# Sharing out the taps of a depthwise convolution: which of GpSimd's products it makes itself, and when VectorE does its own

## The reference, cut to what matters

```python
h = rmsnorm(x, mix_norm)
z = h @ w_in                      # q 1024, k 128, v 128, conv 2 x 1024, gates 2 x 1024
q = partial_rope(rmsnorm(zq.reshape(B, S, 16, 64), q_norm), cos, sin)
k = partial_rope(rmsnorm(zk.reshape(B, S, 2, 64), k_norm), cos, sin)
a = sliding_window_attention(q, k, v, sinks) @ attn_proj

ca, cb = jnp.split(zc, 2, axis=-1)
u = ca * jax.nn.sigmoid(cb)
u = causal_depthwise_conv(u, dw_w, dw_b)       # 31 taps for each of 1024 channels
c = jax.nn.silu(layernorm(u, conv_ln_g, conv_ln_b)) @ conv_proj
merged = jax.nn.sigmoid(ga) * a + jax.nn.sigmoid(gb) * c
x = x + merged @ w_out
```

## Time and profile before

| | before |
|---|---|
| median of 3 runs | 1446.55 us |
| profiled execution, its own time | 1445.92 us |
| its span in the trace | 1444.1 us |
| mean granted clock of TensorE | 0.982 |
| TensorE busy | 1365.7 us (95% of the span) |
| VectorE / ScalarE / GpSimd busy | 961.5 / 786.8 / 141.9 us |
| chain that ended last, by engine | PE 78%, DVE 9%, ACT 6%, DMA 3%, POOL 2% |

### The profile page before, as it was taken

One profiled execution on the slowest core, in us unless ns is written; L12 is line 12 of the kernel. 1 busy time (PEld: TensorE's weight loads), 2 busy tenths in 40 slices (PEclk: granted clock), 3 DMA queues, 4 the chain that ended last, 5 costly groups with the idle time before them and its releaser, 6 DMA issues.

```text
span 1444.1 us, 17190 instructions
## 1 busy us (share of the span) xinstructions
PE 1365.7 (95%) x6482; PEld 1127.0 (78%) x6482; DVE 961.5 (67%) x1397; ACT 786.8 (54%) x1250; POOL 141.9 (10%) x166
## 2 busy tenths in 40 slices
PE   6999999849998999999899999899999999899998
PEld 5788788738876887878778888678888888688886
DVE  4776746797867776774877666648875546665543
ACT  5444447858874654444764444666545664654442
POOL 3000102643430010010001000000000000000000
PEclk9999999969999999999999999999999999999999
DMA  9888755613343588875558876545544344566562
GB/s 256 301 264 274 266 180 167 204 44 103 103 132 110 176 266 264 281 264 181 170 188 273 273 259 188 168 142 162 159 145 118 103 133 160 161 187 183 184 189 87
DMA packets 166691, 269.60 MB, mean 187 GB/s; under 512 B 14096, under 2 KB 114616, under 8 KB 166608
## 3 DMA queue, kind: packets, MB, share of 16 engines
q1 hardware_dynamic: 154240, 226.66, 50.4%
q0 software_dynamic: 12064, 41.49, 8.6%
q10 hardware_dynamic: 304, 0.35, 0.1%
HBM read 267.40 MB, written 1.05 MB: 186 GB/s over the span
## 4 chain that ended last, share of the span: by engine, by line
PE 78%; DVE 9%; ACT 6%; DMA 3%; POOL 2%; issue 2%; SPq 0%; DVEq 0%; ACTq 0%; POOLq 0%
PE ps L1629 25%; PE ps L1608 14%; PE ps L1610 13%; PE ps L1609 13%; DVE w_lo L939 3%; POOL y L485 2%; ACT w_hi L504 2%; PE ps L1784 1%; DMA raw<-in_ffn_wgu_dram 1%; PE ps L2043 1%; PE ps L1678 1%; PE ps L1679 1%; PE ps L1680 1%; PE ps L1696 1%; ACT shift L556 1%
## 5 line engine op out<-in xcount | busy, mean ns | idle before, releaser
L939 DVE TENSOR_TENSOR w_lo<-raw,w_hi 128x1024 fp32r<-128x1024 f32 (+2 forms) x431 | 520.1, 1225 | 285.3 <-ACT w_hi L504 283.7
L504 ACT ACTIVATE w_hi<-raw 128x1024 fp32r<-128x1024 f32 (+2 forms) x431 | 447.9, 1053 | 340.5 <-DMA raw<-in_ffn_wgu_dram 102.6
L1608 PE MATMUL ps<-w_hi,a_hi 128*128 128x512 f32 (+1 forms) x1056 | 426.9, 404 | 9.2 <-DVE a_lo L1094 3.6
L1610 PE MATMUL ps<-w_hi,a_lo 128*128 128x512 f32 (+1 forms) x1056 | 413.8, 392 | 0.0
L1609 PE MATMUL ps<-w_lo,a_hi 128*128 128x512 f32 (+1 forms) x1056 | 413.4, 391 | 0.0
L1608 PEld LDWEIGHTS ps<-w_hi,a_hi 128*128 128x128 f32 x1056 | 200.8, 190 | 48.8 <-DVE w_lo L939 5.3
L1610 PEld LDWEIGHTS ps<-w_hi,a_lo 128*128 128x128 f32 x1056 | 200.6, 190 | 43.0
L1609 PEld LDWEIGHTS ps<-w_lo,a_hi 128*128 128x128 f32 x1056 | 201.2, 191 | 38.1
L1629 PE MATMUL ps<-w_hi,hid_hi 128*128 128x512 f32 x336 | 104.3, 392 | 0.0
L1629 PE MATMUL ps<-w_lo,hid_hi 128*128 128x512 f32 x336 | 103.6, 389 | 0.0
L485 POOL TENSOR_TENSOR y<-y,prod 128x512 f32<-128x512 f32 x60 | 87.6, 1460 | 163.0 <-ACT prod L673 158.6
(11 more groups left out here) (349 smaller groups left out, 1447.0 us busy)
## 6 DMA issues: line engine op xcount, KB each, us to landing
raw<-in_ffn_wgu_dram SPq DMA_DIRECT2D x176, 256.0 KB, 4.3
raw<-in_w_in_dram SPq DMA_DIRECT2D x88, 512.0 KB, 3.7
raw<-in_w_gu_dram SPq DMA_DIRECT2D x176, 256.0 KB, 3.4
ada<-in_w_ada_dram POOLq DMA_DIRECT2D x72, 512.0 KB, 5.6
raw<-in_ffn_wdown_dram SPq DMA_DIRECT2D x44, 512.0 KB, 4.1
raw<-in_w_dn_dram SPq DMA_DIRECT2D x44, 512.0 KB, 3.6
raw<-in_w_in_dram SPq DMA_DIRECT2D x36, 256.0 KB, 3.3
raw<-in_w_out_dram SPq DMA_DIRECT2D x16, 512.0 KB, 3.7
```

Of the source, the lines that this page charges most:

```text
L504: act.activation(w_hi[:, u % RING, 0:nk * n], raw[:, u % RING, 0:nk * n], ACT.Copy).then_inc(hi_ready, 1)
L939: dve.tensor_tensor(w_lo[:, u % RING, 0:nk * n], raw[:, u % RING, 0:nk * n], w_hi[:, u % RING, 0:nk * n].bitcast(F32), ALU.subtract).then_ ...
L1608: pe.matmul(dst(t)[:, 0:n], a[0], slot(u, w_hi, kk, n), start=kc == 0, stop=False)
L1610: i = pe.matmul(dst(t)[:, 0:n], a[1], slot(u, w_hi, kk, n), start=False, stop=kc == KC - 1)
```

## The change

It changes who works on the convolution of the first mixer and in which slots:
- The pairs are exchanged: VectorE has groups 0 and 4 (its first input, `uT` of conv 0, is there one block earlier), GpSimd and ScalarE have 2 and 6.
- For 18 of its 62 taps (first taps included) GpSimd makes both products itself into a buffer of its own, `pown`, and then adds them: taps 5 to 10 of the first pair, and in the second pair every tap with k mod 5 = 2 or 4 (twelve). ScalarE makes the other products (`FED`, 84 of them).
- ScalarE makes 2 products in each of slots 11 to 15, none in 16 to 25, 3 in each slot from 26 on and 3 in each of the first seven steps of the projection.
- VectorE makes 3 instructions of `conv` in slots 7 to 15 (2 in slot 13), none in 16 to 25, 3 in 26 to 30, 4 from 31 on, and 4 in each step of the projection.
- `shape_heads` moves by a slot (third sum in 21, roots in 22, rope in 23, its sums in 24, clearing `kTz` in 25) with counted semaphores in place of some full waits; ScalarE's root and its two table loads move from slot 20 to 21. `gated_conv` moves from the end of a block to the start of the next slot, before that slot's split.
- TensorE's last sums are exchanged: groups 4 and 5 wait for VectorE's taps, then 6 and 7 for GpSimd's.

```diff
-        POOL_CH = [0, 4]
-        VECT_CH = [2, 6]
+        POOL_CH = [2, 6]
+        VECT_CH = [0, 4]
+        POOL_OWN = {(0, k) for k in range(5, 11)} | {(1, k) for k in range(TAPS) if k % 5 in (2, 4)}
+        FED = [(g, k) for g in range(2) for k in range(TAPS) if k > 0 and (g, k) not in POOL_OWN]
...
+            pool.wait_ge(sem("par_ready"), 1)
+            fed = own = 0
             for g in range(2):
                 c = POOL_CH[g]
-                for k in range(1, TAPS):
-                    j = (TAPS - 1) * g + k - 1
-                    pool.wait_ge(sem("conv_product"), TAP2 * g + 2 * (k + 1))
-                    if j >= 1:
-                        pool.wait_ge(sem("pool_step"), j)
-                    pool.tensor_tensor(y[:, c:c + 2, :], y[:, c:c + 2, :], prod[:, j % 2, :, :], ALU.add).then_inc(sem("pool_step"), 1)
+                for k in range(TAPS):
+                    if k == 0:
+                        pool.wait_ge(sem("conv_first"), 2 * (g + 1))
+                        continue
+                    n = (TAPS - 1) * g + k - 1
+                    if (g, k) in POOL_OWN:
+                        own += 1
+                        v = pown
+                        pool.wait_ge(sem("pool_step"), n)
+                        for half in range(2):
+                            pool.tensor_scalar(pown[:, half, :], uT[:, c + half, k:k + S], par[:, c + half, k:k + 1], None, ALU.mult)\
+                                .then_inc(sem("pool_product"), 1)
+                        pool.wait_ge(sem("pool_product"), 2 * own)
+                    else:
+                        v = prod[:, fed % 2, :, :]
+                        fed += 1
+                        pool.wait_ge(sem("conv_product"), 2 * fed)
+                    if n >= 1 and (g, k) not in POOL_OWN:
+                        pool.wait_ge(sem("pool_step"), n)
+                    pool.tensor_tensor(y[:, c:c + 2, :], y[:, c:c + 2, :], v[:, :, :], ALU.add).then_inc(sem("pool_step"), 1)
...
+            def products(n, g_last=1):
+
+                for _ in range(n):
+                    i = made[0]
+                    if i == 2 * len(FED) or FED[i // 2][0] > g_last:
+                        return
+                    g, k = FED[i // 2]
+                    if begun[0] == g:
+                        first_tap(g)
+                        begun[0] += 1
+                    c, j = POOL_CH[g] + i % 2, i // 2
+                    if i % 2 == 0 and j >= 2:
+                        a, b = FED[j - 2]
+                        act.wait_ge(sem("pool_step"), (TAPS - 1) * a + b)
+                    act.activation(prod[:, j % 2, i % 2, :], uT[:, c, k:k + S], ACT.Copy, scale=par[:, c, k:k + 1]).then_inc(sem("conv_product"), 1)
+                    made[0] += 1
...
+            PRODUCTS = {slot: 2 if slot < 16 else 3 for slot in range(11, NMIX) if not 16 <= slot < 26}
...
-                if slot == Q1:
+                if slot == Q1 + 1:
                     load_table(ACT.Sqrt)
...
-                if slot >= 7:
-                    products(3, TAP2 if slot < 27 else 2 * TAP2)
-                if slot == Q1:
+                if slot in PRODUCTS:
+                    products(PRODUCTS[slot], 0 if slot < 30 else 1)
+                if slot == Q1 + 1:
                     act.wait_ge(sem("heads_summed"), 3)
...
             for k in range(KC):
                 w.to(u_ap + k + 4)
-                products(6)
-            products(2 * TAP2)
+                products(3 if k < KC - 1 else 2 * len(FED))
...
-            TAPS_IN = {13: 2, 17: 2, Q1: 2, Q1 + 1: 1, Q1 + 2: 1, Q1 + 3: 1}
+            TAPS_IN = {slot: 0 if slot < 7 or 16 <= slot < 26 else 3 if slot < A0 else 4 for slot in range(NMIX)}
+            TAPS_IN[13] = 2
...
+                if i == 0 and p > 0 and MIX[p - 1][0] == "conv":
+                    gated_conv(p - 1)
                 w.to(M1 + slot + 4)
                 if 1 <= a <= NG:
                     take_values(a - 1)
-                if i == 3 and MIX[p][0] == "conv":
-                    gated_conv(p)
                 if slot in (13, 17):
                     sum_heads(slot // 4 - 3)
-                if Q1 <= slot < Q1 + 4:
+                if Q1 <= slot < Q1 + 7:
                     shape_heads(slot - Q1)
...
-                if slot > 10:
-                    conv(TAPS_IN.get(slot, 3 if slot < Q1 else 4), TAP2 if slot <= 30 else 2 * TAP2)
+                conv(TAPS_IN[slot], TAP2 if slot <= 30 else 2 * TAP2)
             turned_lo("att")
             for k in range(KC):
                 w.to(u_ap + k + 4)
-                conv(6)
+                conv(4)
             conv(2 * TAP2)
...
-            pe.wait_ge(sem("pool_step"), 2 * (TAPS - 1))
+            pe.wait_ge(sem("conv_step"), 2 * TAP2)
             for c in (4, 5):
                 pe.matmul(ps[:, 6, 0:S], ones, y[:, c, :], start=False, stop=False, skip_group_check=True)
-            pe.wait_ge(sem("conv_step"), 2 * TAP2)
+            pe.wait_ge(sem("pool_step"), 2 * (TAPS - 1))
             for c in (6, 7):
```

46 lines of the change are left out of this document (20 added, 26 removed).

## The result

| | before | after |
|---|---|---|
| median (5 runs each) | 1448.75 us (1445.25 to 1452.36) | 1455.62 us (1454.33 to 1460.72) |
| profiled execution, its own time / span | 1445.92 / 1444.1 us | 1455.62 / 1453.8 us |
| VectorE / ScalarE / GpSimd busy | 961.5 / 786.8 / 141.9 us | 964.6 / 773.4 / 181.7 us |

The change makes the kernel slower by 0.6%: ratio 1.0059, 95% interval 1.003 to 1.0088. The forecast was 1442 with a range of 1430 to 1454.

What follows compares the result with a forecast made beforehand. TensorE was taken to be bound by waits for VectorE's cub and kTz copies, caused by ScalarE's products waiting for GpSimd's adds. -23.7 + 5 + 12 + 2 = -4.7 gave a median of 1442 us, range 1430 to 1454.

Steps and rivals of the forecast that it cites:

- front: From the second conv block's cub transposes to the first attention scores: scores at 307.5 instead of 331.2, 23.7 us gained.
- attention, twelve own taps: Attention slots 39 to 43: VectorE operations caught by GpSimd's second-pair own taps, 5 us lost, range 0 to 12.
- part 2: Slots 38 to 43: product 0.65 us, own tap 2.75, two or three VectorE operations caught in odd slots, 5 us lost.
- end: Before the last column sums: TensorE waits 12 us for GpSimd's remaining taps.
- restart at half clock: After 12 us idle TensorE restarts at half clock: sums 0.9 and filling matmuls 1.1 longer, 2 us lost.
- Part 3: The end: ten fed and six own taps plus seven splits take GpSimd 35.3 us against 23.3, so 12 us wait.
- rival of the dear product: GpSimd's second pair: own taps cost more than they save; product 1.0 us gives +6, 1453; chance 0.22.
- Part 1: Slots 16 to 30: ScalarE freed of thirty products, cub at 285, kTz copies at 298.2, scores at 307.5: 23.7 us gained.
- poor front rival: Slots 16 to 30: GpSimd's six own taps still slow VectorE's scaling, gain 19, total 1446; chance 0.14.
- the forecast's own rival: Dear product at 1.0 us, own tap 3.45: attention slots +10, end 16 late; chance 0.22.

Runs made afterwards that it cites:

- e8: Changed kernel, each own tap's two GpSimd products made by one TENSOR_TENSOR of 2x256 columns with the weight broadcast: 1451.2 us, ratio 1.0031 to before.
- e7: Changed kernel, GpSimd's products in 17 of 18 own taps made for 128 columns instead of 256: 1451.49 us, ratio 1.0028 to before.
- e4: Changed kernel without GpSimd's six own taps of the first pair, which are missing from the convolution: 1451.91 us, ratio 1.0033 to before.
- e3: Changed kernel, six of the second pair's twelve own taps moved to the first pair, the other six placed at 2, 5, ... 17: 1450.37 us, ratio 1.0024 to before.
- c7: Changed kernel, own taps only in the first pair (six); ScalarE makes four products in slots 26 to 43; six products and taps per step: 1438.75 us.
- e5: VectorE's part of the change alone: no GpSimd own taps, ScalarE three products in every slot 11 to 43, six per step: 1452.17 us, ratio 1.0039 to before.
- c9: Changed kernel without own taps, three product buffers, six products and taps per step, ScalarE's products and VectorE's taps in other slots: 1439.35 us, ratio 0.9947 to before.
- c10: c7 with VectorE's taps moved forward, so that 18 instead of 31 are left behind slot 43: 1442.59 us, ratio 0.9969 to before.

## Why the prediction was wrong

The order of events was right; the front's gain was taken too large and the end's loss too small, and the sum of small differences turned its sign. By the same stretches:

| term | forecast | measured | why |
|---|---|---|---|
| front | -23.7 | -16.9 | the adds of six own taps held VectorE |
| attention, twelve own taps | +5 | +4.9 | as forecast, see part 2 |
| end | +12 | +18.0 | an own tap is 3.35, not 2.75 |
| restart at half clock | +2 | +2.4 | as forecast |
| sum | -4.7 | +8.4 | |

**Part 3 failed in its price.** The step was "half an add is the nearest row, so 0.65". The product takes 0.92, and beside VectorE 1.10 in the mean. The forecast's 16 taps start at 395.29, 2.7 later than its reckoning (388.66 + 3.9 = 392.6), as GpSimd comes out of the attention slots with own taps undone, and take 433.6 - 395.3 = 38.3 instead of 35.3 (six own taps at 0.6 more each, the seven splits some 0.6 less in all than forecast). These are 5.7 of the 6.0 missing, and e8, at the assumed price, shows a loss of 12.0. The rival of the dear product, whose turning point was 0.85, was the true case; I had weighed 0.22 for it. Halving a row left out that every instruction has a start of its own: e7 against the changed kernel gives 0.32 us for 128 columns more, and so 2.5 ns a column with 0.28 to start. The add has 1.26/512 = 2.5 ns a column with its start in it, so 0.65 was 256 columns at the product's own rate and no start: the 0.28 is what was missing. One input less saves nothing here. The Trainium skill (GPSIMD Engine Reference, Performance versus the Vector engine) allows 1.8 cycles an element at 1.2 GHz to the best one-input loop, an estimate of 0.38 us for 256; the trace does not come near it, 0.915 at the shortest.

**Part 1 failed in its cover.** `cub` at 285 rested on own taps that end near 278, "so the first operations are still blocked" and the rest not. They ended at 284.2, and held VectorE from the split at 265.27 (2.33 us) and the four before the third sum (5.93 us, at 1.21 each 4.9) to the split at 284.54. From the second cub transposes to the third it was to be 285 - 244.0 = 41.0; it was 45.3, and in e4 39.7. Of the 4.3 about 3 were lost before the head scaling began (279.34, forecast 276.5) and 1 behind it. So `cub` came 4 late: the poor front rival (`cub` at 289 to 290) came true beside the dear product. From there to the scores it was 25.0 instead of 22.5, and that is another miss, for e4 has 24.4 there. The way from the `kTz` wait to the scores was taken as 9.3, with "a short wait may or may not cost it" for the slow clock; it was 10.7, as long as before (10.6), with the clock at 0.50 from 303.3 to 308 behind a wait of 3.1. The other 1.1 is the way to the `kTz` copies, 14.3 instead of 13.2. I had given each rival a time with the other term near its forecast. The dear one at 1.0 us, 1453, has a front of 22; with 17 it is 1458, outside the range. Both hang on the same own taps, so they had to be summed. That TensorE would then wait 3.6 for `kTz` was right (3.1), and a cheaper product did not mend the front (69.6 in e7 and e8), as it takes none of the adds away.

**Part 2 was right in its number and its mechanism, but not for the price that it used**: two of VectorE's operations are caught in a slot, at 1.2 us each, and two slots so take 7 us where it was 5.2, a third takes 5.9. e3 prices it again: six own taps more in the attention slots add 5.0. But with a product of 0.92 the forecast's own rival had put attention at +10, and e8, with the cheap product, has +5.5. The product's price hardly counts here, since it is the adds that catch VectorE; that a 5 reckoned from 0.65 held at 0.92 is luck.

**Left out** was what VectorE's own 17 taps more behind slot 43 cost (nothing while GpSimd is last; 3.7 in c7, 8.3 in e5). That ScalarE and VectorE would be paced by GpSimd there was forecast, without a number: ScalarE waited 20.3 us. Two slips in the text did not change the sum: 277.6 - 4 x 2.8 is 266.4 and not 266.6 or 266.8, and GpSimd, said to be done earlier than now, would by the sum itself have been done at 421 and was at 433.6, against 417.4 before.

What stays open is how much of the front's last 6.2 us of waiting for `cub` in c7 a complete kernel can gain: c9, without own taps, has 1.9 there, and pays for it at the end. No run took the adds out of slots 16 to 25 and kept the products there, so that the adds hold VectorE rests on the timelines and on e4, e7 and e8.

## What to carry to other kernels

When work moves to an engine whose price for it no row shows, do not scale a longer instruction down by its columns: its start is in the row too, and each new instruction pays it again. Give the rivals that hang on the same unknown one common case. Work given to GpSimd is paid twice, once in its queue and once by VectorE, which its adds hold up at operations of two columns as much as at large ones; put it where VectorE has nothing urgent, and count what is left of it at the point where its result is needed. Taking a wait away gains nothing where the engine behind it is busy up to the same moment, as ScalarE in c10. A product queue of two buffers ties the maker to the adder: a product that stands behind the adder's own work stops everything else in the maker's queue.

## What the runs showed of the hardware

- GpSimd's `TENSOR_SCALAR` with a weight per partition took 0.60 us for 128 and 0.92 for 256 float32 columns; one `TENSOR_TENSOR` with that weight broadcast made 512 columns in 1.21 (median), 0.6 less than two of the former, but held VectorE, which they did not.
- VectorE's operations on 2 columns took 0.16 us alone and 1.26 beside GpSimd's adds. The Trainium skill (SBUF — State Buffer, Who interferes with whom) has one lock for a whole instruction; both sides of it show between VectorE and GpSimd's adds. With GpSimd's one-input products only one side shows: a pair of 1.83 took 4.25 beside three splits (271.24 us), while no VectorE operation that started during a product was held by more than 0.26.
- After an idle wait of TensorE of 15.5 us (to 429.03) the granted clock was 0.50 from 429 to 435, 0.63 from 435 to 440 and 1.00 from 440 to 445. In c10, after 4.8 us (to 420.67), it was 0.50 from 420 to 425, where c7, without a wait since 415.64, had 1.00. After the wait of 3.14 us for `kTz` in the changed kernel it was 0.50 from 303.3 to 308.
